# Spreading the norms' reciprocals from two fp32r parts instead of from fp32

## The reference

```python
def rms_norm(x, g):
    xf = x.astype(jnp.float32)
    y = xf * lax.rsqrt(jnp.mean(xf * xf, axis=-1, keepdims=True) + EPS)
    return (y * g.astype(jnp.float32)).astype(x.dtype)

def modulate(x, g, shift, scale):
    return rms_norm(x, g) * (1 + scale) + shift
```

## Time and profile before

| | us |
|---|---|
| median of 3 timed runs | 3292.28 |
| lowest and highest of them | 3292.01 to 3294.58 |
| the profiled execution, its own time | 3295.76 |
| its span, first to last instruction | 3294.0 |
| TensorE busy in it | 3215.2 (98%) |
| VectorE, ScalarE busy | 2096.2 (64%), 1210.1 (37%) |

### The profile page before, as it was taken

How to read it: one execution, slowest core, us unless ns; L and a number is a source line. 1 busy time by engine, 2 the same in 40 slices (tenths; PEclk the granted TensorE clock), 3 DMA queues, 4 the chain that set the end, 5 groups by cost and what they waited for, 6 DMA issues and landing times.

```text
span 3294.0 us, 42823 instructions
## 1 busy us (share of the span) xinstructions
PE 3215.2 (98%) x16105; PEld 2691.2 (82%) x16105; DVE 2096.2 (64%) x2917; ACT 1210.1 (37%) x1783; POOL 0.2 (0%) x4
## 2 busy tenths in 40 slices
PE   8989999999999999999999999999999999999998
PEld 5879998887888888888788888888888878888886
DVE  5777886655587778656476555775544676654546
ACT  3654344454232223345332222534222256542221
POOL 0000000000000000000000000000000000000000
PEclk9999999999999999999999999999999999999999
DMA  7564553111334453211223222222222336323222
GB/s 249 185 198 142 186 184 102 65 58 52 121 122 140 162 182 131 96 58 52 77 77 103 100 98 96 79 101 77 96 95 98 104 74 81 63 77 106 93 101 71
DMA packets 100715, 358.24 MB, mean 109 GB/s; under 512 B 11208, under 2 KB 12368, under 8 KB 100560
## 3 DMA queue, kind: packets, MB, share of 16 engines
q1 hardware_dynamic: 98864, 352.92, 32.0%
q10 hardware_dynamic: 1696, 3.16, 2.1%
HBM read 351.83 MB, written 2.10 MB: 107 GB/s over the span
## 4 chain that ended last, share of the span: by engine, by line
PE 90%; DVE 6%; ACT 2%; issue 1%; DMA 1%; DVEq 0%; ACTq 0%; SPq 0%
PE ring L1646 25%; PE ring L1648 25%; PE ring L1647 25%; PE bank L1646 2%; PE bank L1648 2%; PE bank L1647 2%; DVE w_lo L2538 1%; DMA raw<-ws 1%; ACT w_hi L877 1%; PE ring L1737 1%; PE ring L1971 1%; PE ring L1970 1%; PE bank L1995 1%; PE bank L1996 1%; PE ring L1941 1%
## 5 line engine op out<-in xcount | busy, mean ns | idle before, releaser
L1646 PE MATMUL ring<-h_hi,w_hi 128*128 128x512 f32 (+1 forms) x2776 | 1028.8, 371 | 21.9 <-DVE h_lo L2602 12.0
L1647 PE MATMUL ring<-h_lo,w_hi 128*128 128x512 f32 (+1 forms) x2776 | 1020.2, 368 | 0.0
L1648 PE MATMUL ring<-h_hi,w_lo 128*128 128x512 f32 (+1 forms) x2776 | 1020.1, 367 | 0.0
L2538 DVE TENSOR_TENSOR w_lo<-raw,w_hi 128x1024 fp32r<-128x1024 f32 x598 | 730.9, 1224 | 313.9 <-ACT w_hi L877 296.9
L877 ACT ACTIVATE w_hi<-raw 128x1024 fp32r<-128x1024 f32 x598 | 630.5, 1056 | 718.2 <-PE ring L1648 668.2
L1646 PEld LDWEIGHTS ring<-h_hi,w_hi 128*128 128x128 f32 x2776 | 529.5, 191 | 116.0 <-issue 25.0
L1648 PEld LDWEIGHTS ring<-h_hi,w_lo 128*128 128x128 f32 x2776 | 529.1, 191 | 86.0
L1647 PEld LDWEIGHTS ring<-h_lo,w_hi 128*128 128x128 f32 x2776 | 530.1, 191 | 82.6
L1646 PE MATMUL ring<-y_hi,w_hi 128*128 128x512 f32 (+1 forms) x1456 | 540.0, 371 | 10.3 <-DVE z L2817 7.5
L1648 PE MATMUL ring<-y_hi,w_lo 128*128 128x512 f32 (+1 forms) x1456 | 536.5, 368 | 0.0
L1647 PE MATMUL ring<-y_lo,w_hi 128*128 128x512 f32 (+1 forms) x1456 | 536.1, 368 | 0.0
(11 more groups left out here) (371 smaller groups left out, 3110.4 us busy)
## 6 DMA issues: line engine op xcount, KB each, us to landing
raw<-ws SPq DMA_DIRECT2D x614, 512.0 KB, 3.3
z<-ws SPq DMA_DIRECT2D x48, 512.0 KB, 4.4
x<-x_t SPq DMA_DIRECT2D x1, 2048.0 KB, 11.2
out_t<-x SPq DMA_DIRECT2D x8, 256.0 KB, 2.0
z<-xc ACTq DMA_DIRECT2D x6, 256.0 KB, 11.3
xc<-ctx_t SPq DMA_DIRECT2D x1, 1024.0 KB, 8.7
z<-ropes ACTq DMA_DIRECT2D x2, 512.0 KB, 4.1
xc<-xc ACTq DMA_DIRECT2D x2, 256.0 KB, 11.2
```

Source lines behind the costliest of these rows:

```text
L1646: nc.tensor.matmul(o, a_hi, b_hi, start=start, stop=False)
L1647: nc.tensor.matmul(o, a_hi, b_lo, start=False, stop=False)
L1648: return nc.tensor.matmul(o, a_lo, b_hi, start=False, stop=stop)
L2538: nc.vector.tensor_tensor(w_lo[:, u, :], raw[:, u, :], f(w_hi[:, u, :]), ALU.subtract).then_inc(w_ready, 1)
```

## The change

Two new tiles, `rstd_hi` and `rstd_lo`, 128x4 in fp32r. `rstd_parts` makes them on VectorE: the reciprocal as before, then a copy of it to fp32r as the upper part, then reciprocal minus upper part as the lower part; the first two are each waited for, and the third raises the semaphore that TensorE waits for. `spread_parts` makes a spread on TensorE of two fp32r products for each block of tokens, upper and lower part one after the other into the same bank columns, with `ident_r` as moving operand: eight products in place of four fp32 ones (four in place of two for the context). All 16 spreads of the norms go through it. No DMA, no order between the stages and no other wait is changed.

```diff
--- before.py
+++ after.py
@@ -421,6 +421,8 @@
         ones_r = sb("ones_r", [P, P], F32R)
         ident_r = sb("ident_r", [P, P], F32R)
         head_pick = sb("head_pick", [P, P])
+        rstd_hi = sb("rstd_hi", [P, 4], F32R)
+        rstd_lo = sb("rstd_lo", [P, 4], F32R)
         v_bias = sb("v_bias", [P, 8])
         o_bias = sb("o_bias", [P, 8])
         half_b = sb("half_b", [P, 8])
@@ -1709,12 +1711,16 @@
                                              start=k == 0, stop=is_summed or k == KB - 1)
                     m.then_inc(ss_ready, 1)
 
+            def spread_parts(T, spread):
+                for tt in range(T // P):
+                    for part in (rstd_hi, rstd_lo):
+                        m = nc.tensor.matmul(spread[:, tt * P:(tt + 1) * P], part[:, tt:tt + 1].to_broadcast([P, P]),
+                                             ident_r[:, :], start=part is rstd_hi, stop=part is rstd_lo)
+                return m
+
             def spread_rstd(T, spread):
                 pe.wait_ge(s_rstd, C.next(s_rstd))
-                for tt in range(T // P):
-                    m = nc.tensor.matmul(spread[:, tt * P:(tt + 1) * P], rstd_cols[:, tt:tt + 1].to_broadcast([P, P]),
-                                         ident, start=True, stop=True)
-                m.then_inc(s_rspread, 1)
+                spread_parts(T, spread).then_inc(s_rspread, 1)
 
             def blocks_ready(k0):
 
@@ -2209,10 +2215,7 @@
                 ready(first + AB_TILES + 2)
                 mixed(2, range(4, 8))
                 pe.wait_ge(s_ln_rstd, 1)
-                for tt in range(4):
-                    m = nc.tensor.matmul(bank[2][:, tt * P:(tt + 1) * P], rstd_cols[:, tt:tt + 1].to_broadcast([P, P]),
-                                         ident, start=True, stop=True)
-                m.then_inc(s_ln_spread, 1)
+                spread_parts(SEQ, bank[2]).then_inc(s_ln_spread, 1)
                 ready(first + AB_TILES + 3)
                 mixed(3, range(4, 8))
                 for k in range(2):
@@ -2275,10 +2278,7 @@
 
             def deferred_spread():
                 pe.wait_ge(s_rstd, C.next(s_rstd))
-                for tt in range(4):
-                    m = nc.tensor.matmul(bank[0][:, tt * P:(tt + 1) * P], rstd_cols[:, tt:tt + 1].to_broadcast([P, P]),
-                                         ident, start=True, stop=True)
-                m.then_inc(s_h_spread, 1)
+                spread_parts(SEQ, bank[0]).then_inc(s_h_spread, 1)
 
             def ml_in(first):
                 four_abreast(first)
@@ -2559,6 +2559,11 @@
                              lambda k: mod[:, layer, part * KB + k, s:s + 1], None if part else first_main if (layer, stream) == (0, "main") else first_roots(stream),
                              None if part or (layer, stream) != (0, "ctx") else first_shift)
 
+            def rstd_parts(roots, n, made=s_rstd):
+                step(nc.vector.reciprocal(rstd_cols[:, :n], roots))
+                step(nc.vector.tensor_copy(rstd_hi[:, :n], rstd_cols[:, :n]))
+                issue(nc.vector.tensor_tensor(rstd_lo[:, :n], rstd_cols[:, :n], f(rstd_hi[:, :n]), ALU.subtract), made)
+
             def column_rstd(T, kept=None):
                 if kept is None:
                     dve.wait_ge(root_ready, C.next(root_ready, T // P))
@@ -2568,8 +2573,7 @@
 
                     dve.wait_ge(root_ready, C.now(root_ready))
                 roots = root_cols if kept is None else kept
-                nc.vector.reciprocal(rstd_cols[:, :T // P], roots[:, :T // P]).then_inc(s_rstd, 1)
-                C.next(s_rstd)
+                rstd_parts(roots[:, :T // P], T // P)
                 dve.wait_ge(s_rspread, C.next(s_rspread))
 
             def first_shift(k):
@@ -2991,8 +2995,7 @@
                             mod_added(i)
                     if u == 50:
                         dve.wait_ge(root_ready, C.now(root_ready))
-                        nc.vector.reciprocal(rstd_cols[:, :CTX // P], first_roots("ctx")[:, :CTX // P]).then_inc(s_rstd, 1)
-                        C.next(s_rstd)
+                        rstd_parts(first_roots("ctx")[:, :CTX // P], CTX // P)
                     if u == 56:
                         dve.wait_ge(s_rspread, C.next(s_rspread))
                     blocks, lows = CTX_BLOCKS.get(u, ()), CTX_LOWS.get(u, ())
@@ -3249,7 +3252,7 @@
                 nc.vector.tensor_reduce(small[:, 8:12], bank[1][:, 0:16].rearrange("p (b t) -> p t b", b=4), AX_X, ALU.add)\
                     .then_inc(s_var, 1)
                 dve.wait_ge(s_ln_root, 1)
-                nc.vector.reciprocal(rstd_cols, root_cols).then_inc(s_ln_rstd, 1)
+                rstd_parts(root_cols, 4, s_ln_rstd)
                 dve.wait_ge(s_ln_spread, 1)
                 for b in range(5):
                     if b < 4:
@@ -3294,8 +3297,7 @@
                 for u in range(2, 5):
                     lower_w(first + u)
                 dve.wait_ge(root_ready, C.next(root_ready, 4))
-                nc.vector.reciprocal(rstd_cols[:, :], root_cols[:, :]).then_inc(s_rstd, 1)
-                C.next(s_rstd)
+                rstd_parts(root_cols, 4)
                 lower_w(first + 5)
                 lower_w(first + 6)
                 dve.wait_ge(s_h_rstd, i + 1)
```

## The result

| | us | mean of the runs | mean granted clock |
|---|---|---|---|
| kernel before, 11 runs | 3294.58 median (3291.09 to 3296.16) | 3294.0 | |
| changed kernel, 11 runs | 3300.03 median (3294.86 to 3305.69) | 3300.9 | 0.9864 |
| ratio | 1.0019, 95% interval 1.0011 to 1.0027 | | |
| changed kernel's profiled execution | 3300.03, span 3297.9 | | 0.987 |

Slower by 5.45 us between the medians and 6.8 us between the means, where 2.8 was forecast, and above the range's end of 3299.0. The changed kernel's runs also spread more, over 10.8 us against 5.1, and the longest are those with the lowest mean clock: 0.984 for three of the four from 3303.65 to 3305.69, 0.989 for the one at 3294.86.

What follows compares the result with a forecast made beforehand. TensorE, busy 3215.2 of 3294.0 us, was taken as the bound, with serial links at norms. Eight exposed norms 2.76, plus 0.13, less 0.055, gave +2.8 us on 3292.28: 3295.1 us, range 3291.5 to 3299.0.

Steps and rivals of the forecast that it cites:

- the term for the clock: Granted clock at the norms: 0 entered at 502; clock loss at norms with filler left to rival 2.
- TensorE's part: All 16 spreads: eight passes at 0.11 us equal eight records, no throughput saved; last pass releases the bank 0.055 us earlier.
- 1297: Hidden spread at 1297 us, where VectorE waits for TensorE's spread in the chain: gains 0.055 us.
- VectorE's part: Copy and subtraction behind each of 16 reciprocals, 0.20 us each: spread released 0.40 us later, bounds 0.36 to 0.54.
- 2910: Norm whose reciprocal starts at 2909.62, partly covered by filler until 2910.16: +0.13 us.
- hidden spreads: L2213, three of L2279, those at 1226 and 1297: VectorE's 0.40 us covered by TensorE's products, smallest cover 2.0 us.
- The sum of the chain: Eight exposed norms at +0.345 us make 2.76, plus 0.13 at 2910, less 0.055 at 1297: +2.8 us.
- The term for 502: Spread at 502.56, before the clock falls to 0.50: slower loads +0.3 us at most, half regained; entered 0.
- Rival 2: Longer idle drops the clock at filler norms: two norms or more 3301.9 us, chance 0.06; one 3298.5, chance 0.04.
- Rivals 1 and 3: 1: fast passes, eight take 0.48 us, 3290.0, chance 0.07; 3: delay lost behind norms, 3292.6, chance 0.07.
- The base: Median of three timed runs of the kernel before, 3292.28 us, to which +2.8 was added.

Runs made afterwards that it cites:

- The upper part alone: Lower part left out, four one-pass products for a spread and no operation added on VectorE; against the kernel before, -9.4 +- 1.6 us in six runs.

## Why the prediction was wrong

The step that failed is the term for the clock. The forecast entered 0 at 502, since TensorE would only start its product later in the same slow stretch, had no term at the last norm, and left the norms with filler to a rival of small chance. In its place the runs show 3.8 us above the chain (6.9 +- 1.7 less 3.1), more than the chain itself, and put it down to the longer idle ahead of the spreads, with a smaller part by a mere shift not excluded. The steps one by one:

- **TensorE's part: right.** A pass is 0.11 us apart from the next, by its load; the throughput is that of the fp32 records, and the last pass frees the bank 0.05 us earlier (1297: 3.64 to 3.59). Whether the fp32 records stood on their load too, as the prediction says, or on two streams of 0.06 us each, no run separates; both make their 0.11. The upper part alone, with 0.11 us for each pass left out, shows the price from the other side. The halving that a count of passes promises (the Trainium skill, "FP8 and Floating Point Precision", TensorE Precision Notes) is not in the time; the rule on the load (the Trainium skill, "TensorE: Matmul & The Clock Gate", LDWEIGHTS) agrees with these 0.11 us.
- **VectorE's part: right.** Links of 0.21 and 0.20 us, reciprocal to spread 0.63, reciprocal to read 1.78, and each fully exposed norm without a slow stretch 0.35 or 0.36 us longer for 0.345. At 2910 it is 0.15 for 0.13. The links of the hidden spreads cost nothing.
- **The sum of the chain: nearly right.** Six norms 2.13, 502 and the last 0.69 (at the forecast's 0.345 each, since slow stretches lie over them), 2910 0.15, 1297 -0.05, and the five hidden spreads 0.03 each, for which the forecast had 0: 3.1 us for 2.8.
- **The term for 502: wrong.** I saw that the clock fell there and entered 0, since TensorE's product would start later in the same slow stretch. The stretch itself became longer: 10 us at 0.50 in place of 6.7 in four of the six traces with the links at this norm and no filler there, and 2.0 to 2.3 us more than before in place of 0.35. The other two have 6.8 us (417.8 and 418.0 for norm and stage). Without links there it is 10 us in one of seven traces.
- **Rival 2: had the mechanism, and too small a chance.** It gave 10% to the loss of the clock at a norm with filler, priced a whole stretch at 3.4 us and looked only at those norms. The traces show smaller pieces at more places: 0.6 to 1.3 us at a norm with filler, in some executions and at different norms; 1.7 at 502 in four traces of six; and 0.9 at the last norm, which has three filler matmuls and which I had not counted. All four traces with the links and these three matmuls have that 0.9, but so have two of the seven without links there, the kernel before among them. How much of the 3.8 us falls to each place isn't shown.
- **Rivals 1 and 3: not so.** Eight passes took 0.84 us (2314.96 to 2315.80) and not 0.48; the single 0.06 is that of the first pass behind a wide product. And a delay arrives at the end: the 3.0 us put in at 312 made the program 4.4 +- 1.7 us longer.
- **The base.** I worked from the median of the three runs shown, 3292.28; eleven runs gave 3294.58, and 107 a mean of 3295.2. These 2.3 us are nearly half of the 4.9 by which the time was missed. With the right base the sum is 3297.4, 2.6 below the median of the changed kernel; between the means the loss is 4.0 us more than the 2.8 forecast.

What stays open: why twice the links cost hardly more than once, why leaving out the lower part won 3 us more than its passes, how large a part a mere shift has, and how the loss by the clock divides among the norms over many executions, since a trace is one execution only. That the idle ahead of the spreads makes a loss is shown by the kernel that has less filler and nothing else (+3.3 +- 1.8), and by the one with all eight passes and without the links (+0.1 +- 1.3). That the loss is the clock's fits with the filler at 502, under which the links cost 3.8 +- 1.5 us, about their chain.

## What to carry to other kernels

A product that waits for its weights' load gains nothing from fewer passes while the number of loads stays the same, as here, with two for each block before and after; with half the loads (the upper part alone) it did gain. So compare the distance of starts for the same load at two widths, before a product is split. Two tiny operations on another engine cost their 0.2 us each at every place where the first engine waits, and they can cost as much again through the clock (here 3.8 us on top of 3.1): look at the granted clock at each such place, also where it is still 1.00, and ask how much idle it stands. Start what can start (here the upper part) and make the rest beside it. And take several traces before a slow stretch is put down to a change: the kernel before has them too, not always at the same places.

## What the runs showed of the hardware

- A 128x128 load holds one-pass products of 128 columns 0.11 us apart at a clock of 1.00, also when all its columns are one broadcast element, and 0.21 us at 0.50, where the load's own record takes 0.33 us for 0.19: the load goes by the same clock.
- VectorE starts a second small operation that waits for nothing 0.09 us after the first (919.72, 919.81), where one that waits for the semaphore of the operation before it starts after 0.20 (919.69, 919.89).
- Time and mean clock of an execution go together: over the 107 runs of the kernel before, 0.001 less of mean clock goes with 2.1 us more, with a correlation of -0.64. So a run's mean clock tells a part of why it was long, not all.
- Taking two filler matmuls away ahead of each spread, 0.46 us of idle more at each of these norms, cost 3.3 +- 1.8 us.
